# Full-width turns and numerators for the new tokens, and the state's products two pairs at a time, in a YOCO mLSTM / MoBA decoder step

## Time and profile before

| | |
|---|---|
| three timed runs | 907.96, 909.8 and 910.47 us; median 909.8 |
| span of the profiled execution, first to last instruction | 909.7 us |
| TensorE matmul (PE) busy | 896.8 us, 99% |
| TensorE weight load (PEld) busy | 838.1 us, 92% |
| DVE / ACT / POOL busy | 622.7 / 438.1 / 64.7 us |
| mean granted TensorE clock | 0.996 |
| HBM traffic | 175.24 MB read, 6.32 MB written |

### The profile page before, as it was taken

One profiled execution on the slowest core, in us unless ns is written; L12 is line 12 of the kernel. 1 busy time (PEld: TensorE's weight loads), 2 busy tenths in 40 slices (PEclk: granted clock), 3 DMA queues, 4 the chain that ended last, 5 costly groups with the idle time before them and its releaser, 6 DMA issues.

```text
span 909.7 us, 18709 instructions
## 1 busy us (share of the span) xinstructions
PE 896.8 (99%) x7472; PEld 838.1 (92%) x7472; DVE 622.7 (68%) x1089; ACT 438.1 (48%) x826; POOL 64.7 (7%) x81
## 2 busy tenths in 40 slices
PE   9999999999999999999999999999999999999996
PEld 8999988999999999999888878987999999999985
DVE  6477568788976575677575847446578897757536
ACT  5445666476345363445344453345447644526421
POOL 0010006500000000330000000000230000000000
PEclk9999999999999999999999999999999999999999
DMA  9982215664454444566988997998944545454401
GB/s 285 265 250 95 94 48 138 188 196 140 140 178 146 139 142 159 167 219 231 334 292 282 360 373 283 399 400 352 284 144 144 179 132 195 148 169 148 139 1 59
DMA packets 132331, 182.78 MB, mean 201 GB/s; under 512 B 5875, under 2 KB 113211, under 8 KB 132244
## 3 DMA queue, kind: packets, MB, share of 16 engines
q1 hardware_dynamic: 126938, 177.56, 59.0%
q0 software_dynamic: 640, 2.10, 0.9%
q10 hardware_dynamic: 4666, 1.92, 0.8%
HBM read 175.24 MB, written 6.32 MB: 200 GB/s over the span
## 4 chain that ended last, share of the span: by engine, by line
PE 94%; DMA 2%; SPq 1%; ACT 1%; DVE 1%; issue 1%; DVEq 0%
PE ps L624 24%; PE ps L626 23%; PE ps L625 23%; PE ps L1019 7%; PE ps L1061 4%; PE ps L1119 2%; DMA page<-in_cache_v_dram 2%; PE ps L907 1%; PE ps L909 1%; PE ps L908 1%; SPq L535 1%; SPq L542 1%; DMA x_tok<-in_x_prompt_dram 1%; PE ps L638 1%; PE ps L741 0%
## 5 line engine op out<-in xcount | busy, mean ns | idle before, releaser
L1232 ACT ACTIVATE w_hi<-raw 128x1024 fp32r<-128x1024 f32 x192 | 202.4, 1057 | 227.2 <-PE ps L626 204.4
L1636 DVE TENSOR_TENSOR w_lo<-raw,w_hi 128x1024 fp32r<-128x1024 f32 x192 | 237.4, 1240 | 102.7 <-ACT w_hi L1232 102.6
L624 PE MATMUL ps<-x_hi,w_hi 128*128 128x322 f32 (+1 forms) x888 | 279.8, 315 | 0.0
L626 PE MATMUL ps<-x_hi,w_lo 128*128 128x322 f32 (+1 forms) x888 | 276.5, 311 | 0.0
L625 PE MATMUL ps<-x_lo,w_hi 128*128 128x322 f32 (+1 forms) x888 | 276.1, 311 | 0.0
L624 PEld LDWEIGHTS ps<-x_hi,w_hi 128*128 128x128 f32 x888 | 168.1, 189 | 5.2 <-ACT k_turned L1523 2.9
L624 PE MATMUL ps<-h_hi,w_hi 128*128 128x320 f32 x552 | 170.9, 310 | 0.0
L626 PE MATMUL ps<-h_hi,w_lo 128*128 128x320 f32 x552 | 170.5, 309 | 0.0
L625 PE MATMUL ps<-h_lo,w_hi 128*128 128x320 f32 x552 | 170.4, 309 | 0.0
L625 PEld LDWEIGHTS ps<-x_lo,w_hi 128*128 128x128 f32 x888 | 168.8, 190 | 0.2
L626 PEld LDWEIGHTS ps<-x_hi,w_lo 128*128 128x128 f32 x888 | 167.6, 189 | 0.0
(11 more groups left out here) (347 smaller groups left out, 978.7 us busy)
## 6 DMA issues: line engine op xcount, KB each, us to landing
raw<-in_w_up_dram SPq DMA_DIRECT2D x32, 1024.0 KB, 5.8
raw<-in_w_down_dram SPq DMA_DIRECT2D x32, 1024.0 KB, 5.2
page<-in_cache_k_dram SPq DMA_DIRECT2D x64, 512.0 KB, 5.7
page<-in_cache_v_dram SPq DMA_DIRECT2D x64, 512.0 KB, 9.4
raw<-in_w_in_a_dram SPq DMA_DIRECT2D x11, 1024.0 KB, 8.7
raw<-in_w_kv_dram SPq DMA_DIRECT2D x8, 1024.0 KB, 6.6
raw<-in_w_out_a_dram SPq DMA_DIRECT2D x4, 1024.0 KB, 5.2
raw<-in_w_q_b_dram SPq DMA_DIRECT2D x4, 1024.0 KB, 5.4
```

Of the source, the lines that this page charges most:

```text
L624: mm(out, WH[PLACE[t]][:, k, :], hi[:, k, 0:width], start=(k == 0), stop=False)
L626: last = mm(out, WL[PLACE[t]][:, k, :], hi[:, k, 0:width], start=False, stop=(k == 7))
L1232: A(WH[PLACE[t]][:, :, :], raw_tile(t), ACT.Copy)\
L1636: V.tensor_tensor(WL[PLACE[t]][:, :, :], raw_tile(t), WH[PLACE[t]][:, :, :].bitcast(F32), ALU.subtract)\
```

## The change

The new tokens' blocks are brought to 128 rows and columns, and the state's products are made in two visits instead of four.

```diff
@@ TensorE, x turned
+            pe.wait_ge(s_gz, 1)
-                nc.tensor.transpose(bank[:, 256:320], XS[0:64, 2, c], ident[0:64, 0:64]).then_inc(s_xt, 1)
+                nc.tensor.transpose(bank[:, 256:384], XS[:, 2, c], ident).then_inc(s_xt, 1)
@@ TensorE, numerator(h)
-                mm(bank[r, 260:389], w[:, 384:448], VT[:, 2, h, :], start=False, stop=True, skip_group_check=True)\
+                mm(bank[:, 260:389], w[:, 320:448], VT[:, 2, h, :], start=False, stop=True, skip_group_check=True)\
                     .then_inc(s_num, 1)
@@ TensorE, turned_back(h)
+                if h == 0:
+                    pe.wait_ge(s_p, 4)
                 if h >= 1:
                     pe.wait_ge(s_hg, h)
+                nc.tensor.transpose(ps[5][:, 192:320], HN[h % 2][:, 2, :], ident)
                 nc.tensor.transpose(ps[5][:, 0:128], HN[h % 2][:, 0, :], ident)
-                nc.tensor.transpose(ps[5][:, 128:256], HN[h % 2][:, 1, :], ident)
-                nc.tensor.transpose(ps[5][:, 256:320], HN[h % 2][r, 2, :], ident[r, r]).then_inc(s_bk, 1)
+                nc.tensor.transpose(ps[5][:, 128:256], HN[h % 2][:, 1, :], ident).then_inc(s_bk, 1)
@@ TensorE, state_step(n)
-                if 2 <= n < 6:
-                    j = n - 2
+                for j in {3: (0, 1), 5: (2, 3)}.get(n, ()):
                     pe.wait_ge(s_wk, 8)
                     pe.wait_ge(s_hg, H)
                     pe.wait_ge(s_vm, j + 1)
@@ ACT normalised(h) and DVE divisors(h)
-                r, bank, d = slice(64 * (h % 2), 64 * (h % 2) + 64), ps[6 + h % 2], rd[h % 2]
+                r, bank, d = SAMPLE_ROWS, ps[6 + h % 2], rd[h % 2]      # slice(64, 128)
@@ DVE, at the start (and the waits for s_gz of 1 become 2)
+            V.memset(XS[64:128, 2, :], 0.0).then_inc(s_gz, 1)
             V.memset(WG[:, :, :].bitcast(F32), 0.0).then_inc(s_gz, 1)
@@ DVE, state(n) and its call in the loop over the w_out tiles
-                if n >= 3:
-                    j = n - 3
+                if n >= 4:
+                    j = n - 4
...
-                if n < 6:
+                if n < 7:
                     state(n + 1)
@@ POOL, at the start
             own(G.memset(XL[:, 7, 0:T].bitcast(F32), 0.0))
+            for hn in HN:
+                own(G.memset(hn[0:64, 2, :], 0.0))
             own(G.memset(aqZ[:, :, :, :], 0.0))
```

More of the change, by code:

```diff
@@ L386, in build @@
         s_co, s_po = sem("c_stored"), sem("prompt_state_stored")
+        SAMPLE_ROWS = slice(64, 128)
         SCORE_BANK = (4, 7, 5, 6)
@@ L751, in numerator @@
             def numerator(h):
-                r, w, bank = slice(64 * (h % 2), 64 * (h % 2) + 64), W[h % 3], ps[6 + h % 2]
+                w, bank = W[h % 3], ps[6 + h % 2]
                 pe.wait_ge(s_W, h + 1)
@@ L763, in numerator @@
                 mm(bank[:, 130:259], w[:, 256:384], VT[:, 1, h, :], start=False, stop=True, skip_group_check=True)
-                mm(bank[r, 260:389], w[:, 384:448], VT[:, 2, h, :], start=False, stop=True, skip_group_check=True)\
+                mm(bank[:, 260:389], w[:, 320:448], VT[:, 2, h, :], start=False, stop=True, skip_group_check=True)\
                     .then_inc(s_num, 1)
             def turned_back(h):
-                r = slice(64 * (h % 2), 64 * (h % 2) + 64)
                 pe.wait_ge(s_hn, h + 1)
+                if h == 0:
+                    pe.wait_ge(s_p, 4)
                 if h >= 1:
                     pe.wait_ge(s_hg, h)
+                nc.tensor.transpose(ps[5][:, 192:320], HN[h % 2][:, 2, :], ident)
                 nc.tensor.transpose(ps[5][:, 0:128], HN[h % 2][:, 0, :], ident)
-                nc.tensor.transpose(ps[5][:, 128:256], HN[h % 2][:, 1, :], ident)
-                nc.tensor.transpose(ps[5][:, 256:320], HN[h % 2][r, 2, :], ident[r, r]).then_inc(s_bk, 1)
+                nc.tensor.transpose(ps[5][:, 128:256], HN[h % 2][:, 1, :], ident).then_inc(s_bk, 1)
             pe.wait_ge(s_col, 1)
@@ L1250, in _ @@
             act.wait_ge(s_gw, 16)
-            act.wait_ge(s_gz, 1)
+            act.wait_ge(s_gz, 2)
             A(WG[:, :, 0:8], wgraw[:, :, 0:8], ACT.Copy)
@@ L1658, in _ @@
                     dve.wait_ge(s_gh, 1)
-                    dve.wait_ge(s_gz, 1)
+                    dve.wait_ge(s_gz, 2)
                     V.tensor_tensor(WG[:, :, 64:72], wgraw[:, :, 0:8], WG[:, :, 0:8].bitcast(F32), ALU.subtract)
@@ L1756, in divisors @@
                     dve.wait_ge(s_hn, h - 1)
-                r, bank, d = slice(64 * (h % 2), 64 * (h % 2) + 64), ps[6 + h % 2], rd[h % 2]
+                r, bank, d = SAMPLE_ROWS, ps[6 + h % 2], rd[h % 2]
                 dp, ds = bank[:, 128:259:130], bank[r, 388:389]
```

## The result

Timed against the kernel before on the same chip, the changed kernel takes 913.51 us (median of 20 runs, 910.76 to 915.69) against 910.47 us (20 runs). The ratio is 1.0037, 95% interval 1.0028 to 1.0046: slower by 2.5 to 4.2 us. The forecast was 910.9 us, +1.1 us and no measurable difference, with 912.8 as the upper end.

The account below looks back on a forecast made before the run. TensorE sets the end for 94% of the span. On the span of 909.7 us, turns of x -0.24, heads -1.94, tail +0.4 and state +2.9 give +1.1, 910.8, median 910.9 us; 8-in-10 range 907.9 to 912.8.

Parts of the forecast that it names:

- Turns of x: Turning x at the start, 0.33 us a chunk instead of 0.57: gain 0.24 us, bounds 0 and 1.9.
- Heads: Passes 2 to 6, where full-width products and turns back shorten TensorE's stream: gain 1.94 us, bounds 1.4 and 2.1.
- halves for product and turn back: In pass 4 the 0.59 us gained is split: 0.30 us to the product, half to the turn back.
- Tail: End of the heads, divisors to ACT to turn back, all heads now in rows 64 to 127: +0.4 us, bounds 0 and 0.6.
- The wait for pair 1: Second double visit, behind w_out tile 5, waits for DVE's later additions of pair 1: +1.9 us in place of -0.7.
- the contention: POOL's sums of tile 3 run beside DVE's low part of weights and get longer: +1.0 us, bounds 0 and 1.2.
- The merged visit: Making the state's products in two visits instead of four saves 0.7 us in all, if no wait arises.
- The clock: Rival, chance 0.20: granted clock falls in the new wait of the second double visit, +1.7 us, giving 912.6 us.
- the forecast's own list of signs of being wrong: Second double visit without a gap, granted clock under 1 near it, or pair 1's additions ended before TensorE comes.
- no contention: Rival, chance 0.15: POOL's sums end at 146.57 as before, giving 909.9 us.
- the second visit doesn't wait: Rival, chance 0.10: DVE adds pairs 0 and 1 earlier, the state's part is -0.7 us, giving 907.3 us.
- widening does nothing: Rival, chance 0.05: a narrow instruction's lateness belongs to what stands before it, so no gain, giving 912.8 us.

Follow-up runs that it names:

- experiment 2: The kernel before with only the two double visits for the state's products, nothing widened: 914.96 us, ratio 1.0067.
- experiments 8 and 9: The kernel with the widening alone, one operation narrow again: first the turn back (907.5 us), then instead the numerator's last product (910.04 us); one execution each.
- experiment 7: The kernel before, all operations as narrow, with every head's new tokens in rows 64 to 127; one execution, 911.24 us.
- experiment 3: The changed kernel with 14 extra unused matmuls on TensorE before pair 3's wait: 911.38 us, ratio 1.0011 to the kernel before.
- experiment 4: The changed kernel with DVE's low part of weights in iteration 3 held until POOL's first sums are made: 911.49 us, ratio 1.0006 to the kernel before.
- experiment 12: The changed kernel with joined divisors and DVE adding pairs 0 and 1 in iteration 3, ahead of x_low(3): 905.65 us, ratio 0.9956 to the kernel before.
- experiment 5: The changed kernel with DVE adding pairs 0 and 1 in iteration 3, ahead of x_low(3): 908.56 us, ratio 0.9973 to the kernel before.

## Why the prediction was wrong, point by point

- **Turns of x** (-0.24, bounds 0 and 1.9): right. A chunk comes every 0.33 us (7.73, 8.06, 8.39), and TensorE then waits 1.06 us for x_lo. From the landing of the first weight tile to the last gate products it takes 13.01 - 10.65 = 2.36 us, 13.40 - 10.80 = 2.60 before: -0.24. Against experiment 2, which also has the old turns, it is -0.38.
- **Heads** (-1.94): measured -1.94 us. The halves for product and turn back hold in pass 4 (experiments 8 and 9).
- **Tail** (+0.4, bounds 0 and 0.6): +0.70, over the upper bound. The cause named, rows 64 to 127, is shown by experiment 7 (+0.64). The size is short at turn back 6: from B it comes 124.81 - 117.97 = 6.84 us later, 128.11 - 121.83 = 6.28 before, so +0.56 where the forecast has +0.3. Of the 0.26 us more, 0.19 is the start of the chain: the divisors of head 5 should have begun 0.13 us earlier and begin 0.06 later (119.60 - 117.97 = 1.63, 1.57 before), since DVE's low part of weights lies in the way (118.47 to 119.68). Head 7's round adds 0.14, forecast 0.1.
- **The wait for pair 1** (+1.9) **and the contention** (+1.0): +2.88 us together in experiment 3, 1.02 of it contention in experiment 4. TensorE reaches the second visit 150.27 - 131.17 = 19.10 us after C; the forecast's 153.4 is 19.07 after it. The Trainium skill (GPSIMD Engine Reference, Key points) has VectorE operations with two SBUF inputs get in GpSimd's way; 1.88 us beside the low part and 0.86 without it agree. One reading of the earlier trace rows was wrong, though: the 1.86 us isn't "the one place" where the sums meet a low part. In the kernel before, the low part of 146.05 meets two sums; it takes 1.61 us instead of 1.21, the first sum its usual 0.86 and the second 1.18. So either engine can be the one that pays, and the forecast gave no reason why it should be the sum; that part of the +1.0 was luck. DVE's timeline before, then POOL's:

```profile
146.05 1.61 DVE L1636 TENSOR_TENSOR w_lo<-raw,w_hi 128x1024 fp32r<-128x1024 f32 x1
...
145.71 0.86 POOL L2249 TENSOR_TENSOR sum_xx<-sq,sq 128x320 f32<-128x320 f32 x1
147.22 1.18 POOL L2248 TENSOR_TENSOR sum_x<-sum_x,x 128x320 f32<-128x320 f32 x1 [0.64 <-ACT sq L1385]
```

- **The merged visit** (-0.7 for two): -0.37 for each where nothing waits (experiment 12).
- **The clock: the step that failed.** The forecast's own case leaves the granted clock at 1.00 in the new wait and puts the fall among the rivals, with 0.20 and +1.7 us. It fell, as the forecast's own list of signs of being wrong has it, and cost 3.11 us (experiment 3), a term that the sum had at nothing. Two arguments gave way. "Each piece of waiting is short": it took a single wait of 2.06 us, between products of 32x32 weights, and one of 1.46 us did it too. "The pair's products between them are the same as in the visits of before, which saw no drop": those stood between dense tiles, with no pause beside them, and even double visits keep 1.00 where nothing waits (experiment 5). And the rival's price was read off, where 5 x 0.34 = 1.7 us of full speed are lost, 3.4 us at half clock; here it was 6.8 us at half clock. (As time the stretch of the earlier trace rows is worth 1.5 us and not 1.7, by the stages.) With the fall at its measured price the sum is +1.1 + 3.1 + 0.3 for the tail = +4.5 us. The rule that was cited with this rival (the Trainium skill, TensorE: Matmul & The Clock Gate, What's actually happening: the slow clock is the default and activity releases it) agrees with the trace: 0.50 behind the wait, and 1.00 again from about 161.8, with TensorE at work since 153.84. It gave no reason for a chance as small as 0.20.
- **Rivals refuted:** no contention (experiment 4), the second visit doesn't wait (2.06 us), widening does nothing (-1.94 us).
- **The base of the sum:** 909.8 us was the median of three executions; that of 20 is 910.47. So of the 2.6 us between 913.51 and the forecast 0.7 are the base, and 1.9 are the difference (+3.0 by the medians, +1.1 forecast). "The median lies 0.1 above the span" was chance. The profiled execution of before took its slow stretch of 1.5 us, and other profiles' own times lie about 1.8 us over their spans. The difference isn't touched by that, since both kernels are timed over many executions.

What stays open: why the slow stretch at 45 us stands in some executions and not in others, and whether the drop behind the new wait is in all of the changed kernel's executions. The mean granted clock of each execution is on record: 15 of the changed kernel's 20 have 0.992 to 0.995, under all 12 of experiment 3 (0.996 to 0.999), so they lost more clock than any with the wait filled; for the other five (0.996 and 0.997) it can't be told. +3.4 us measured against +4.3 by stages would fit a drop that is shorter or missing in some. Which waits bring a fall isn't settled either: one of 1.46 us between 32x32 products did, those of 0.8 and 1.3 us between full ones didn't.

## What to carry to other kernels

- A wait that a reordering makes on TensorE can cost twice: once for its length, and once for the clock behind it. Here 2.9 us of lateness brought another 3.1 us by half clock, and 14 matmuls of no use, put in the wait, kept the clock up.
- Before work of two steps is merged into one visit, look at who gives its buffers back and in which place of that engine's order. The merge was worth 0.37 us a visit; the additions one iteration later cost 2.9, of which 1.0 is the low part of weights that now ran beside POOL's sums.
- In a chain that goes round three engines, small instructions are worth joining, even into wider ones, and worth starting at row 0. From divisors to ACT it is 1.11 us with six operations that take the 64 rows from row 64, 0.75 with six that take them from row 0, and 0.59 with three on 128x3. With ACT's third copy on all rows as well the tail became 2.4 us shorter.

## What the hardware showed that was not expected

- **Instructions for rows 64 to 127 behind ones for all rows.** On ACT the copy of 64 rows starts 0.37 to 0.38 us behind a copy of 128 rows (121.33 behind 120.95), the copy of 128 rows in its place 0.25 us (120.63 behind 120.38). Half the rows, half as much time again. It is where the rows begin, not how many they are: in the kernel before the copy of rows 0 to 63 of head 6 starts 0.25 us behind too (127.70 behind 127.45). On DVE each of the pair (128x2, 64x1) starts 0.16 to 0.20 us behind the other; from row 0 the 64x1 starts 0.07 to 0.09 us behind the 128x2 (126.51 behind 126.44). That makes the 0.75 us of the earlier trace rows. Why the start row matters no run here shows.
- **A clock drop outlasts its cause.** The wait ended at 153.84; the granted clock fell only at 155, when TensorE was busy again, and came back at about 161.8, inside tile 6, which ends at 162.5.
- **One program, two courses.** The slow stretch at 45 us is there (0.66 to 0.78 over 45 to 50 us, since it begins earlier in some) or not (1.00) in profiles of kernels whose code up to there is the same, and is worth 1.5 us of span each time.
